# A two-layer decoder trunk: blocks 8 and 9 of layer 0 become a pair, and layer 0's modulation pieces are dealt out anew

## The reference

```python
mod = jax.nn.silu(c) @ w_ada + b_ada
sh1, sc1, gt1, sh2, sc2, gt2 = [m[:, None, :] for m in jnp.split(mod, N_MOD, axis=-1)]
h = _rmsnorm(x, g_pre_mix) * (1.0 + sc1) + sh1
proj = h @ w_in
...
x = x + gt1 * _rmsnorm(mixed @ w_out, g_post_mix)
h = _rmsnorm(x, g_pre_ffn) * (1.0 + sc2) + sh2
f = (jax.nn.silu(h @ w_gate) * (h @ w_up)) @ w_down
return x + gt2 * _rmsnorm(f, g_post_ffn)
```

## Time and profile before

| | us |
|---|---|
| median of 3 runs | 842.99 (842.76 to 843.09) |
| profiled execution: its own time | 842.83 |
| its span in the trace | 841.0 |
| TensorE busy | 831.0 (99%) |
| VectorE busy | 687.9 (82%) |
| ScalarE busy | 459.0 (55%) |
| POOL busy | 119.3 (14%) |

### The profile page before, as it was taken

The page is one execution under the profiler, slowest core; times in us unless marked ns, Lnnn a source line. Parts: engine busy times, 40 slices in busy tenths (PEclk is TensorE's granted clock), DMA queues, the critical chain, the costliest instruction groups (busy, mean ns, idle before and its releaser), DMA issues.

```text
span 841.0 us, 11584 instructions
## 1 busy us (share of the span) xinstructions
PE 831.0 (99%) x4131; PEld 689.2 (82%) x4131; DVE 687.9 (82%) x1180; ACT 459.0 (55%) x732; POOL 119.3 (14%) x92
## 2 busy tenths in 40 slices
PE   8999999999999999999999999999999999999997
PEld 6877888888888888888888788888888788788885
DVE  5898889888787777787689899988787887989984
ACT  5675555565657433434476555465565745454542
POOL 5500300301210012030320040040040000000002
PEclk9999999999999999999999999999999999999999
DMA  8996666576317788777437756766643396165362
GB/s 347 404 368 237 212 262 249 202 268 233 130 73 297 277 285 314 277 290 301 173 126 283 290 207 222 264 219 242 240 146 118 146 347 233 51 258 192 150 226 75
DMA packets 34795, 194.09 MB, mean 231 GB/s; under 512 B 4273, under 2 KB 4529, under 8 KB 17714
## 3 DMA queue, kind: packets, MB, share of 16 engines
q1 hardware_dynamic: 33410, 189.64, 61.0%
q0 software_dynamic: 1328, 3.71, 1.3%
HBM read 192.29 MB, written 1.05 MB: 230 GB/s over the span
## 4 chain that ended last, share of the span: by engine, by line
PE 92%; DMA 3%; DVE 2%; issue 1%; ACT 1%; SPq 0%; DVEq 0%
PE ps L1735 24%; PE ps L1737 23%; PE ps L1736 23%; PE ps L2154 5%; PE ps L1848 4%; DMA wide_t<-scale_first 3%; PE ps L1912 2%; PE ps L1772 1%; PE ps L1773 1%; PE ps L1779 1%; PE ps L1933 1%; PE ps L1934 1%; PE ps L1894 1%; PE ps L1911 1%; PE ps L1932 1%
## 5 line engine op out<-in xcount | busy, mean ns | idle before, releaser
L1156 DVE TENSOR_TENSOR w_lo<-raw,w_hi 128x2048 fp32r<-128x2048 f32 (+2 forms) x126 | 288.2, 2294 | 55.4 <-ACT w_hi L769 54.1
L1735 PE MATMUL ps<-w_hi,t_hi 128*128 128x512 f32 (+2 forms) x712 | 282.0, 396 | 1.6 <-DVE w_lo L1156 1.0
L1737 PE MATMUL ps<-w_hi,t_lo 128*128 128x512 f32 (+2 forms) x712 | 275.1, 386 | 0.0
L1736 PE MATMUL ps<-w_lo,t_hi 128*128 128x512 f32 (+2 forms) x712 | 274.5, 386 | 0.0
L769 ACT ACTIVATE w_hi<-raw 128x2048 fp32r<-128x2048 f32 (+2 forms) x128 | 240.5, 1883 | 33.0 <-DMA raw<-w_stream 26.9
L666 POOL PARTITION_ALL_REDUCE wide_t<-wide_t x20 | 77.0, 3849 | 591.7 <-DVE wide_t L1281 590.8
L1735 PEld LDWEIGHTS ps<-w_hi,t_hi 128*128 128x128 f32 x712 | 133.8, 188 | 30.4 <-DVE w_lo L1156 2.9
L1737 PEld LDWEIGHTS ps<-w_hi,t_lo 128*128 128x128 f32 x712 | 133.7, 188 | 27.6
L1736 PEld LDWEIGHTS ps<-w_lo,t_hi 128*128 128x128 f32 x712 | 134.0, 188 | 25.1
L1281 DVE SCALAR_TENSOR_TENSOR wide_t<-ada,cs,wide_t 128x1024 f32<-128x1024 f32 x80 | 110.2, 1378 | 0.4
L1735 PE MATMUL ps<-w_hi,m_hi 128*128 128x512 f32 x208 | 84.6, 407 | 0.3 <-DVE m_lo L1455 0.3
(11 more groups left out here) (257 smaller groups left out, 1072.9 us busy)
## 6 DMA issues: line engine op xcount, KB each, us to landing
raw<-w_stream SPq DMA_DIRECT2D x124, 1024.0 KB, 5.4
ada<-w_ada SPq DMA_DIRECT2D x80, 512.0 KB, 5.8
wide_t<-gains POOLq DMA_DIRECT2D x7, 512.0 KB, 4.6
mixed<-w_stream SPq DMA_DIRECT2D x3, 1024.0 KB, 8.5
raw<-w_stream SPq DMA_DIRECT2D x4, 656.0 KB, 6.8
mixed<-scale_first SPq DMA_DIRECT2D x2, 1024.0 KB, 10.3
wide_t<-shift_first SPq DMA_DIRECT2D x4, 512.0 KB, 10.9
wide_t<-scale_first SPq DMA_DIRECT2D x2, 1024.0 KB, 12.5
```

The costliest lines, as they stand in the source:

```text
L1156: nc.vector.tensor_tensor(w_lo[:, U % RING, a:n], src[:, a:n], w_hi[:, U % RING, a:n].bitcast(F32), ALU.subtract).then_inc(s_lo, 1)
L1735: nc.tensor.matmul(dst, hi, w_h, start=first, stop=False)
L1736: nc.tensor.matmul(dst, hi, w_l, start=False, stop=False)
L1737: return nc.tensor.matmul(dst, lo, w_h, start=False, stop=last)
```

## The change

Blocks 8 and 9 of layer 0 become a pair. The pieces of layer 0 (0, 2, 3, 3, 3, 3, 3, 3, 2, 2, 0 in blocks 0 to 10) come 2, 4, 4, 4, 4, 2 in blocks 0 to 5, none in 6 and 7, and 4 in the pair; the two `make_table` stand behind blocks 3 and 5 instead of 4 and 8. In a single block with four pieces, VectorE takes one ahead of the gate products and one between them, instead of two ahead. SyncE's code isn't changed. Layer 1 is left as it is, and so is the mixer.

```diff
-TWINS = ((), (5, 8))
+TWINS = ((8,), (5, 8))
@@ def ffn_pieces(l):
     if l + 1 < DEPTH:
-        return (0, 2, 3, 3, 3, 3, 3, 3, 2, 2, 0), (4, 8)
+        return (2, 4, 4, 4, 4, 2, 0, 0, 4, 0, 0), (3, 5)
@@ block.vector, single blocks
                     for u in ahead[:1]:
                         split_lo(l, u)
-                    add_pieces(max(many - 2, 0))
+                    add_pieces(many > 2)
...
                         gate_m(l, j, t, ps[:, QKT + t, 256:512])
+                        if t == 0:
+                            add_pieces(max(many - 3, 0))
```

## The result

| | before | changed |
|---|---|---|
| median, us (range) | 843.04 (842.76 to 843.12) | 866.30 (865.11 to 867.28) |
| profiled execution, us | 842.83 | 866.06 |
| its span, us | 841.0 | 864.3 |

The changed kernel is slower: its time is 1.0276 times that of before, 95% interval 1.0265 to 1.0288. The forecast was 858.4 us, in a range of 846 to 867: the measured median lies inside it, 0.7 us from its upper end. First the page of the changed kernel, busy time and chain of waits, beside the earlier trace rows, and from its fifth part the group of TensorE's turns (line, engine, operation, count, then busy and mean, then idle time just before).

The account below looks back on a forecast made before the run. The prediction took TensorE, busy for 99% of the span, as the bound: 842.8 - 2.7 + 0.5 + 4.2 + 9.8 + 1.0 + 2.8 = 858.4 us, with a range of 846 to 867.

Parts of the forecast that it names:

- the pair: Blocks 8 and 9 of layer 0: 96 up-product matmuls become 84, counted in full as -2.7 us.
- VectorE in blocks 2 to 7: Some 25 us more VectorE work in layer 0, mostly hidden in its free time: +0.5 us, from 0 to 2.
- block 1's waits: Layer 0, block 1: TensorE waits for the second gate product behind piece 3's late load: +4.2 us, 3.7 to 6.6.
- block 10's wait: Layer 0, block 10's first turn: late loads at the pair's end +9.8 us, plus +1.0 for the split beside POOL.
- clock: TensorE's clock falls after two waits, 1.4 us charged for each: +2.8 us, from 0 to 8.
- I charge nothing for: Block 1's `w_down` unit, issued 5 us later or more behind piece 3, wanted some 15 us on: no charge.
- The end of the pair: Last unit, piece 23 and the 1312-column unit are issued late in the queue, so TensorE waits before block 10: +9.8 us.
- POOL's part: POOL's sum of the last part runs beside the 1312-column split that TensorE waits for: +1.0 us, from 0 to 2.
- From 0 to 2 us; I take 0.5, near the rows of layer 1: Charge for VectorE's added work in layer 0's blocks 2 to 7, as layer 1 carries the same sums without TensorE waiting.
- VectorE as the bound in blocks 4 to 7: Rival: POOL sums, table, token sums and additions use up VectorE's slack, 2 to 4 us on top, 861 to 862; chance 0.05.
- Free: Rival: the pair costs no wait and the queue hides everything, 840.1 us, faster than before; chance 0.11.
- Only the first wait: Rival: block 1 waits, but piece 22 and the last unit come in time at the pair's end, 846.2 us; chance 0.06.

Follow-up runs that it names:

- experiment 4: Changed kernel with a third piece buffer for pieces 0 to 19 of layer 0's FFN (blocks 0 to 5): 859.53 us.
- experiment 3: Changed kernel with VectorE taking block 1's first two pieces behind the second gate product in layer 0, loads unchanged: 868.56 us.
- experiment 1: Changed kernel with only SyncE's order altered: layer 0's last unit issued ahead of the pair's third piece, the fourth piece moved into block 10's list: 856.64 us.
- experiment 2: Changed kernel with the pair's pieces spread: 20 and 21 issued ahead of its units and used early, 22 and 23 issued behind them: 854.71 us.
- experiment 5: Changed kernel with block 5's token sums behind the second gate product: 867.84 us; with ScalarE's copy also moved behind both splits: 862.92 us.
- experiment 8: Several combinations; the one with waits 1.36 + 1.09 is the changed kernel with pieces spread, third piece buffer, and block 5's sums and copy moved: 847.59 us.
- the run with fillers: Changed kernel with 80 products that nobody reads on TensorE in front of block 10's first turn: 865.84 us.

## Why the prediction was right in sign and short in size

The steps of the sum, each against the two traces:

| step | predicted | measured | |
|---|---|---|---|
| the pair | -2.7 | -2.0 | 12 matmuls fewer, but the pair's 84 start 0.229 us apart and not 0.227 (0.2), and a stop of 0.3 lies between the pair's two turns; 0.2 open |
| VectorE in blocks 2 to 7 | +0.5 | +3.1 | block 5's wait, clock apart |
| block 1's waits | +4.2 | +3.9 | 1.21 + 2.69 |
| block 10's wait | +10.8 | +12.2 | with the split beside POOL |
| clock | +2.8 | +5.3 | three stops instead of two, 2.4 + 1.6 + 1.3 |
| restarts, layer 1 | 0 | +0.8 | what the others leave of 23.3 |

The range of 846 to 867 held by 0.7 us, and one of the four runs (867.28) lies above it; that it held owes something to luck, since block 5's term was wrong. Of the 7.7 us that the sum was short of the span's 23.3, block 5's wait has 2.6, the clock 2.5, block 10's wait 1.4, the pair 0.7 and the unnamed rest 0.8, and block 1 takes 0.3 off.

**Block 1 was right**, the mechanism to the instruction: the third piece waits for a load that the queue holds until piece 1 is used (experiment 4 takes the cause away and with it the wait for the DMA). Two things beside it were not seen. Block 0's last piece and block 1's first stand together ahead of the first gate product, so this one is late too; it is all that is left in experiment 4. And "I charge nothing for" the unit behind the piece was wrong: VectorE stood 2.80 us for it in the changed kernel, and 4.36 in experiment 3, where TensorE felt it.

**The end of the pair was right** in every link, by experiments 1 and 2. The last unit took 5.97 us to land, as worked out; piece 23 took 3.83 instead of 3.4 and the 1312-column unit 5.19 instead of 4.8. From the last unit's issue to the end of the gate product it was 21.3 us instead of 20.2, and TensorE ran dry 9.2 us after that issue, not 10.4: I had laid layer 1's clock over a layer that reaches the pair's end otherwise. The two make the 2.4 us between 9.8 and 12.2. POOL's part was a row by itself and was smaller in the first split (2.02 us where 2.5 was forecast).

**The step that failed** is "From 0 to 2 us; I take 0.5, near the rows of layer 1". Block 5 cost 4.9 us with its clock. VectorE's free 5.4 us in a block were counted as an average; the token sums, 5.1 us, stand between the two gate products, where TensorE gives about 2 us of room, and ScalarE's copy waits for them in order and holds back the next high part. Experiments 4 and 5 show both halves: with units in time the wait shrinks, with sums and copy moved it all but goes. Why layer 1 bears the same order can be read from the two traces. In the kernel before, layer 1, the sums begin 6.95 us before TensorE comes to the turn:

```profile
688.53 2.29 DVE L1189 TENSOR_TENSOR token_sums<-t_hi,t_lo 128x2048 f32<-128x2048 f32 x1
...
695.48 0.60 PE L1848 MATMUL ps<-const,ffn_m 128*128 128x128 f32 x4
```

In the changed kernel, layer 0, block 5, they begin 2.13 us before it:

```profile
342.59 2.29 DVE L1189 TENSOR_TENSOR token_sums<-t_hi,t_lo 128x2048 f32<-128x2048 f32 x1
...
344.72 0.38 PE L1850 MATMUL ps<-const,ffn_m 128*128 128x128 f32 x2
```

In experiment 4 it is 4.11 us. Lead and wait add up to 5.2 us in both kernels that wait (2.13 + 3.08, 4.11 + 1.07), the time of the sums; layer 1's lead is longer than that, so it has no wait. What the prediction took over from layer 1 was the work, and not how far ahead of TensorE VectorE comes to it. In the changed kernel VectorE is late because the unit for the split ahead of block 5's first gate product lands only at 338.10, with ScalarE waiting 2.61 us for it. Its buffer was free from 324.97, but in the queue it stood behind a piece's load that had to wait until the piece between block 4's gate products was used, at 327.70; it left at 328.10 and took 10.0 us, the DMA engines being busy for 0.97 to 1.03 of the time from 330 to 338 us. POOL's sum slowed VectorE in block 4, but only after that load had left, and VectorE waits 0.56 us again before that split, so the sum doesn't explain the lateness.

The rival "VectorE as the bound in blocks 4 to 7", which had a chance of 0.05, had the right place and with 2 to 4 us nearly the right size (block 5 took 4.9 with its clock), but it is the order of the work more than its amount: experiment 5 has the same amount and 0.3 us of waiting there.

**The clock** was mis-sized: 1.4 us a stop against 2.4, 1.6 and 1.3, and there was a third stop. The granted clock in these traces: after 1.21 + 2.69, 3.08 and 12.23 us of waiting it was 0.50, after 1.29 + 1.09 (experiment 4) and after 1.82 + 0.28 (experiment 1) it stayed at 1.00. That is a part of what experiment 4 paid beyond its forecast. But the length of a stop doesn't settle it: after 1.36 + 1.09 (experiment 8) and 0.86 + 1.09 (experiment 2) the clock fell to 0.50, and after 3.11 us in block 5 of experiment 3 it stayed at 1.00. What does settle it stays open.

**The rivals.** "Free" (840.1) is what the best kernel here comes within 3 us of, but only with a third buffer, another dealing of the pieces, and another order in SyncE's queue, ScalarE's program and the pair. "Only the first wait" (846.2) is like experiments 1 and 2 in shape and 8.5 to 10.4 us too low, for block 5, the clock and what is left of the waits at the end.

## What to carry to other kernels

In a queue that issues in order, a load that must wait for its buffer delays every load behind it: count for each wait what stands behind it, not only what it is for; here the order of a few issues was worth 10 us and the sum of twelve matmuls 2. An engine's free time per block says nothing about an insertion between two results that another engine waits for: ask how much room is left at that very place, and which third engine waits in order for the inserted work. And when work is dealt anew, follow each count that something else hangs on (here the sixteenth piece, on which a sum, a load and a table hang).

## What was not expected of the hardware

- Behind its three stops of 3 to 12 us in the changed kernel TensorE ran 6 to 12 matmuls at the lower level, and the longest stop had the fewest. In that one the granted clock was 0.50 from 431 us on, so most of the lower level passed while TensorE stood; in block 5 it was still 0.98 between 348 and 349, and 0.50 only after the restart. Stops of nearly the same length had both outcomes: after 1.36 + 1.09 us (experiment 8) it was 0.50, after 1.29 + 1.09 (experiment 4) 1.00, and after 3.11 us (experiment 3, block 5) 1.00. In the run with fillers, which kept it busy for 9.86 us of the wait, the granted clock was 1.00 between 440 and 445 us.
- VectorE beside a POOL sum was slowed, not shut out. Splits of 1312 columns took 2.02 and 3.21 us (1.52 at 30.90 in the kernel before, where POOL did nothing; the 1.52 of the earlier trace rows had begun 0.26 us ahead of a POOL sum and lost nothing), operations on 2048 columns 2.60 to 4.31 (2.29 alone), a piece 3.26 (1.28 alone), the gate product between two of them 0.41 as ever. The Trainium skill, "SBUF — State Buffer", section "SBUF: two separate sides", has the two exclude each other for the whole instruction. Here the first split started at 438.69, 1.6 us after the first of POOL's two sums had begun. The first sum ended at about 440.4, and by that rule the split would have ended 1.5 us after it, at 441.9; it ended at 440.71, having lost 0.5 us. The profile's times on POOL are rough.
